# Reading GpSimd's column numbers straight from a table in memory, in a hybrid encoder block

## The chip, the cores and the metric

One core of a Trainium2 chip runs the whole kernel. The metric is the device time of one execution in microseconds; of several runs the median stands. The profile is one further execution, taken by the hardware profiler. TensorE multiplies, VectorE and ScalarE work on PSUM and SBUF, GpSimd works on SBUF, SyncE issues most transfers. Each engine has a sequencer that runs its instructions in order; register work (loads of registers, bounds checks, additions) is done by the sequencer itself.

## The reference

The kernel computes one layer of an encoder block on 512 tokens of width 2048, in float32. What matters here is its last part, a mixture of experts:

```python
h = rmsnorm(x)                                   # 512 x 2048
# top-1 of 4 groups, then top-2 of 8 experts in it: 1024 picks (token, expert, gate)
for e in range(32):                              # w_gate, w_up: 2048 x 512, w_down: 512 x 2048
    y = (silu(h[tokens_of(e)] @ w_gate[e]) * (h[tokens_of(e)] @ w_up[e])) @ w_down[e]
    x[tokens_of(e)] += gate * y
```

Before it come a combined projection, sliding-window attention, a multi-scale pool, an output projection and a cross-attention to 256 memory tokens. None of that is touched. Which tokens an expert gets is known only at run time.

## The kernel before

**Blocks.** The picks are sorted into blocks of 64 slots, block `b` for expert `b` (`SLOTS = 64`, `NE = 32`); up to 16 more blocks would take what doesn't fit, and a count `more` says how many there are. For a block, TensorE multiplies the 64 gathered columns `xsT` with gate and up (64 matmuls, `gate_up`, L2258), turns the result, and multiplies with down (32 matmuls, `down`, L2284). Two blocks make a pair; even blocks use columns 0 to 63 of `xsT` (`par` 0), odd ones 64 to 127. After a pair, a one-hot matrix spreads its results over the tokens (L2217) and VectorE adds them to the residual (L1647).

**Weights.** An expert is 6 units of 2 MB (`expert_unit`; 0 and 2 gate, 1 and 3 up, 4 and 5 down). SyncE loads each into its place in a ring as soon as TensorE has used what was there (`load_units`, L521). The fourth unit of block 0 goes, in three pieces, to buffers that only become free when the routing tables are done (`first_up`, L515, behind the semaphore `table_ready`).

**The columns.** `H` holds the normed activations, transposed: token `t` is one column of 16 values on each of 128 partitions. The gather is a copy of that column, with the token number in a register: 64 copies of 128x16 a block. For each group of 32 copies the sequencer loads 32 registers by one instruction (`TENSOR_LOAD`), then does for each register one fused operation and one bounds check (64 instructions, L695 "ISA x64" below), then issues the copies (L700, each with one more register operation). Blocks 0 and 1 are shared: ScalarE copies columns 0 to 31 (L1096), GpSimd columns 32 to 63, from `first_row`, a row of 128 token numbers that VectorE writes first (`first_ids`). From block 2 on GpSimd does all of it, alone, in a loop over pairs (L725): it fetches the pair's 128 numbers from `ids_dram`, a table in memory, to `first_row` in SBUF by a DMA (L719), waits for its landing, and does four groups of 32. Before the first copy of a block it waits until the block before the previous one has left `xsT` (`gu_copied`). TensorE's `gate_up` waits for the whole block (`block_rows`). The table itself is written once, by a DMA of GpSimd (L711), behind VectorE's `ids_ready`.

**The tables.** VectorE makes them in one sequence: the numbers of the first pair (L1597), the table `ids` (L1623), the weights of the picks (L1628), the list for blocks beyond 32 (L1631 to L1636), and copies of the gates, the last of which raises `table_ready` (L1639). TensorE fills its waits there with matmuls on constants (`keep_busy`, L1746).

Of the kernel before, what the change touches and what calls it, by code (L numbers as in the profile page):

```python
# [58 lines left out]
CUT = 3  # L59


def hybrid_block(nc, x, mem, mix_norm_g, w_in, q_norm_g, k_norm_g, sink_logits, pool_w, pool_scale,
# [5 lines left out]
    with ExitStack() as ctx:  # L68
# [104 lines left out]
        xsT = PB[:, 0:KD * P].rearrange("p (k n) -> p k n", n=P)  # L173
        first_up = [PB[:, 4096:6144], kx[:, :, :].rearrange("p h n -> p (h n)"), vx[:, :, :].rearrange("p m n -> p (m n)")]
# [3 lines left out]
        last_act_t = PB[:, 8704:8704 + KF * SLOTS]  # L178
# [45 lines left out]
        first_up_in = sem("first_up_in")  # L224
        first_used = sem("first_halves_used")
# [112 lines left out]
        pair_ids_in = sem("pair_ids_in")  # L338
# [136 lines left out]
        def _(sp):  # L475
# [34 lines left out]

            sp.wait_ge(table_ready, 1)
# [24 lines left out]
            with sp.Fori(2, NE - 2) as b:  # L536
                load_expert(b, b)
# [34 lines left out]
        def _(pool):  # L572
# [119 lines left out]
            def copy_columns(tokens, par, first, done, free=None):  # L692

                for at in range(first, SLOTS, 32):
                    _, where = nc.values_load_multi_w_load_instructions(  # L695
                        tokens[:, at:at + 32], engines=(mybir.EngineType.Pool,), min_val=0, max_val=S - 1)
                    if at == 0:
                        pool.wait_ge(gu_copied, free)
                    for j in range(32):
# [5 lines left out]
            for par in range(2):  # L705
                copy_columns(first_row[0:1, par * SLOTS:(par + 1) * SLOTS], par, 32, first_rows[par])
# [3 lines left out]
            pool.wait_ge(ids_ready, 1)  # L710
            pool.dma_start(ids_dram.rearrange("j (e s) -> (j e) s", e=2), ids[:, :]).then_inc(ids_stored, 16)  # L711
# [1028 lines left out]
        def _(pe):  # L1740
# [453 lines left out]
            def expert_landed(b, u):  # L2194
# [3 lines left out]
                else:  # L2198
# [3 lines left out]
                    if u < 2 and not (isinstance(b, int) and b < 1):  # L2202
                        loads += 1
# [220 lines left out]
```

## Time and profile before

| | us |
|---|---|
| median of 3 runs | 1741.24 (1740.82 to 1741.37) |
| the profiled execution | 1744.3 |
| its span | 1742.5 |
| mean granted TensorE clock | 0.953 |
| TensorE busy | 1530.3 (88%) |
| VectorE busy | 601.1 (34%) |
| GpSimd busy | 450.8 (26%) |
| ScalarE busy | 365.7 (21%) |

The span lies 1.8 us under the execution's own time. TensorE's busy time counts matmuls from issue to a modelled end, so 88% doesn't mean that it works at its peak. Register and DMA-issuing instructions aren't counted as busy, which matters for GpSimd: they appear as `POOLq`, its sequencer, in the chain and in the list of one line's instructions. Lines such as L695 are those of the listing above. The experts' part begins at about 686 us of the span.

### The profile page before, as it was taken

To read this page: it belongs to the slowest core of one execution; us is meant where nothing else is said; L and a number is where in the kernel's file an instruction comes from. 1 tells how busy PE (TensorE), PEld (TensorE's weight loads), DVE (VectorE), ACT (ScalarE), POOL (GpSimd) and SP (SyncE) were. 2 spreads that over 40 slices of the span, in tenths; PEclk is the share of its full clock that TensorE was granted. 3 is DMA by queue.
4 is the path that set the end of the run, shared out by engine and by line. 5 is a ranking of instruction groups with operands and counts; after the bars stand their busy time and mean duration, and the time that the engine had idled before them with its cause. 6 is when DMAs were issued, how large, how long until landed. Compare 5 with 4: busy or idle time off the path is not lost.

```text
span 1742.5 us, 25966 instructions
## 1 busy us (share of the span) xinstructions
PE 1530.3 (88%) x7008; PEld 868.5 (50%) x7008; DVE 601.1 (34%) x726; ACT 365.7 (21%) x705; POOL 450.8 (26%) x2198
## 2 busy tenths in 40 slices
PE   7999999999999998887977977977977977987977
PEld 7787777588885666232332332332332332332323
DVE  6655666632234335021221221221321231221214
ACT  6422334522222443201001001010010110010101
POOL 4560073400000000332232233233233233233230
PEclk9999999999999999998988988988999998998989
DMA  8433222542222114899999999999999998999984
GB/s 291 112 82 96 81 65 73 195 102 97 97 97 97 49 49 197 335 429 395 409 375 379 415 374 375 411 379 377 406 380 379 411 378 357 412 376 375 411 337 194
DMA packets 88922, 472.66 MB, mean 271 GB/s; under 512 B 5026, under 2 KB 43084, under 8 KB 62924
## 3 DMA queue, kind: packets, MB, share of 16 engines
q1 hardware_dynamic: 87800, 470.84, 67.8%
q0 software_dynamic: 880, 0.35, 0.4%
q14 instruction: 108, 0.88, 0.1%
q8 instruction: 34, 0.56, 0.1%
q10 hardware_dynamic: 100, 0.03, 0.0%
HBM read 466.99 MB, written 4.21 MB: 270 GB/s over the span
## 4 chain that ended last, share of the span: by engine, by line
PE 36%; POOLq 22%; issue 18%; POOL 12%; DMA 6%; DVE 4%; ACT 2%; SPq 0%; DVEq 0%; ACTq 0%
POOLq L695 20%; POOL proj_buffer L700 12%; PE ps L1965 10%; PE ps L1839 9%; DMA proj_buffer<-block_ids 4%; PE ps L2018 3%; PE ps L2258 3%; POOLq L700 1%; DMA weight_ring<-in_xkv_w_dram 1%; PE ps L1801 1%; PE ps L2348 1%; PE ps L2081 1%; ACT weight_ring L889 1%; PE ps L1894 1%; PE ps L2217 1%
## 5 line engine op out<-in xcount | busy, mean ns | idle before, releaser
L2258 PE MATMUL ps<-weight_ring,proj_buffer 128*64 128x512 f32 x2032 | 480.8, 629 | 134.6 <-POOL proj_buffer L700 134.6
L700 POOL COPY proj_buffer<-transposed_acts 128x16 f32 x1984 | 300.9, 214 | 666.1 <-issue 607.4
L2258 PEld LDWEIGHTS ps<-weight_ring,proj_buffer 128*64 128x64 f32 x2032 | 181.5, 145 | 429.0 <-issue 405.8
L1647 DVE TENSOR_TENSOR residual<-ps,residual 128x1024 f32<-128x1024 f32 x128 | 150.8, 1220 | 346.4 <-PE ps L2217 345.6
L2284 PE MATMUL ps<-weight_ring,proj_buffer 128*64 128x512 f32 x960 | 214.2, 599 | 19.5 <-DVE proj_buffer L1657 18.5
L1663 DVE SCALAR_TENSOR_TENSOR y_low<-ps,proj_buffer,y_high 64x1024 fp32r<-64x1024 f32 x60 | 77.0, 1283 | 236.7 <-ACT y_high L1082 235.7
L2284 PEld LDWEIGHTS ps<-weight_ring,proj_buffer 128*64 128x64 f32 x960 | 68.0, 138 | 148.2 <-issue 145.2
L1071 ACT ACTIVATE proj_buffer<-ps 128x512 f32<-128x512 f32 x32 | 19.1, 598 | 531.3 <-PE ps L2258 531.3
L1082 ACT ACTIVATE y_high<-ps,proj_buffer 64x1024 fp32r<-64x1024 f32 x60 | 66.5, 1109 | 289.9 <-PE ps L2284 289.2
L1839 PE MATMUL ps<-mix_high,w_in_high 128*128 128x512 f32 x288 | 117.3, 407 | 1.3 <-issue 1.3
L1839 PE MATMUL ps<-mix_high,w_in_low 128*128 128x512 f32 x288 | 112.3, 390 | 0.0
L1839 PE MATMUL ps<-normed_low,w_in_high 128*128 128x512 f32 x288 | 112.3, 390 | 0.0
L1965 PE MATMUL ps<-weight_high,mix_high 128*128 128x512 f32 x256 | 99.8, 390 | 1.0 <-issue 1.0
L1965 PE MATMUL ps<-weight_low,mix_high 128*128 128x512 f32 x256 | 99.6, 389 | 0.0
L2217 PE MATMUL ps<-y_high,spread 128*128 128x512 f32 x240 | 85.8, 439 | 9.3 <-DVE residual L1647 9.3
L1657 DVE TENSOR_TENSOR proj_buffer<-proj_buffer,ps 128x256 f32<-128x256 f32 x32 | 13.3, 416 | 197.6 <-ACT proj_buffer L1075 197.6
L2217 PE MATMUL ps<-y_low,spread 128*128 128x512 f32 x240 | 75.1, 394 | 0.0
L689 POOL MEMSET memory_values<- 128x160 f32 x1 | 0.2, 232 | 282.6 <-PE ps L2063 282.6
L1197 DVE TENSOR_TENSOR w_in_low<-weight_ring,w_in_high 128x1024 fp32r<-128x1024 f32 x36 | 48.0, 1337 | 69.7 <-ACT w_in_high L812 69.6
L2217 PEld LDWEIGHTS ps<-y_high,spread 128*128 128x128 f32 x240 | 37.0, 188 | 53.1 <-DVE residual L1647 37.1
L1360 DVE TENSOR_TENSOR weight_low<-weight_ring,weight_high 128x1024 fp32r<-128x1024 f32 x32 | 38.5, 1224 | 70.1 <-ACT weight_high L939 70.1
L1839 PEld LDWEIGHTS ps<-mix_high,w_in_high 128*128 128x128 f32 x288 | 54.1, 188 | 15.0 <-issue 3.9
(322 smaller groups left out, 1814.9 us busy)
## 6 DMA issues: line engine op xcount, KB each, us to landing
weight_ring<-in_expert_w_down_dram SPq DMA_DIRECT2D x63, 2048.0 KB, 12.1
weight_ring<-in_expert_w_gate_dram SPq DMA_DIRECT2D x62, 2048.0 KB, 10.3
weight_ring<-in_expert_w_up_dram SPq DMA_DIRECT2D x61, 2048.0 KB, 15.6
weight_ring<-in_w_in_dram SPq DMA_DIRECT2D x18, 1024.0 KB, 5.6
weight_ring<-in_w_out_dram SPq DMA_DIRECT2D x16, 1024.0 KB, 5.0
weight_ring<-in_xkv_w_dram SPq DMA_DIRECT2D x8, 1024.0 KB, 7.7
residual<-in_x_dram SPq DMA_DIRECT2D x8, 1024.0 KB, 12.9
weight_ring<-in_xq_w_dram SPq DMA_DIRECT2D x4, 1024.0 KB, 9.8
```

What stands on the lines that cost most here:

```text
L695: _, where = nc.values_load_multi_w_load_instructions(tokens[:, at:at + 32], engines=(mybir.EngineType.Pool,), min_val=0, max_val=S - 1)
L700: ins = g.tensor_copy(xsT[:, :, par * SLOTS + at + j], H[:, :, ds(where[j], 1)].rearrange("p k n -> p (k n)"))
L1082: a.activation(high[par * SLOTS:(par + 1) * SLOTS, 2 * side:2 * side + 2, :], ps[rows, 4:6, :], ACT.Copy, scale=gate[rows, ds(b, 1)]).then ...
L1197: v.tensor_tensor(in_lo[:, half], raw, in_hi[:, half].bitcast(F32), ALU.subtract).then_inc(w_lo_ready, 1)
L1647: v.tensor_tensor(part, ps[:, bank:bank + 2, :].rearrange("p b n -> p (b n)"), part, ALU.add).then_inc(signal, 1)
L1663: v.scalar_tensor_tensor(out=low[par * SLOTS:(par + 1) * SLOTS, 2 * side:2 * side + 2, :], in0=ps[rows, 4:6, :], scalar=gate[rows, ds(b, 1 ...
L1839: ins = mm(ps[:, bank, :].rearrange("p (t n) -> p t n", n=P), w_[:, half, kk, :], h_, start=(k == 0 and part == 0), stop=(k == KD - 1 and ...
L1965: ins = mm(ps[:, 4 * (n % 2) + t, :], m_, w_[:, r, kk, :], start=(u % 8 == 0 and kk == 0 and part == 0), stop=(u % 8 == 7 and kk == 1 and ...
L2018: ins = mm(ps[:, 4 + t % 2, :], H[:, k, t * P:(t + 1) * P], w[:, kk, :], start=(k == 0), stop=(k == KD - 1))
L2217: ins = mm(ps[:, bank + n, :], onehot[:, t * P:(t + 1) * P], y[:, 2 * side + n, :], start=(start and y is high), stop=(stop and y is low))
L2258: ins = mm(ps[side * SLOTS:(side + 1) * SLOTS, 0, :], xsT[:, k, par * SLOTS:(par + 1) * SLOTS], gate_up_weights(e, u, kk), start=(k == 0), ...
L2284: ins = mm(ps[half, 4 + n % 2, :], act_t[:, f * SLOTS:(f + 1) * SLOTS], w[:, n * 512:(n + 1) * 512], start=(f == 0), stop=(f == KF - 1), s ...
```

## The change

Four things change.

1. In the loop over pairs GpSimd no longer brings the numbers to SBUF. Each group of 32 loads its registers from the table in memory; the compiled program first loads the table's address, adds the offset, and loads the numbers. The semaphore `pair_ids_in` goes.
2. Columns of block 0 are shared among three engines: ScalarE 26, VectorE 12, GpSimd 26. Of block 1, ScalarE copies 28 and GpSimd 36. VectorE's 12 stand between the weights of the picks and the list for further blocks, so ahead of `table_ready`. GpSimd's store of the table moves from behind both blocks to between them.
3. Loads: the first half of block 1's first gate unit goes to a free buffer (`second_gate`) as soon as the activations are turned (`h_turned`); half of block 2's first gate unit gets a semaphore of its own, and block 2's loads are written out ahead of the loop. `last_act_t` moves to the memory of `H`.
4. `keep_busy` ahead of block 0 issues 20 matmuls on constants instead of 6.

```diff
+BY_ACT, BY_DVE = 26, 12
...
+        second_gate = PB[:, 2048:4096]
...
-        last_act_t = PB[:, 8704:8704 + KF * SLOTS]
+        last_act_t = Hf[:, 0:KF * SLOTS]
...
+            sp.wait_ge(h_turned, 56)
+            sp.dma_start(second_gate, expert_unit(1, 0)[:, 0:CHK]).then_inc(half_gate_in[0], 16)
             sp.wait_ge(table_ready, 1)
...
-            for half in range(2):
-                for u in range(2):
-                    if half == 0:
-                        sp.wait_ge(first_used, u + 1)
-                    else:
-                        sp.wait_ge(used, UE + u + 1)
-                    sp.dma_start(unit(u)[:, half * CHK:(half + 1) * CHK], expert_unit(1, u)[:, half * CHK:(half + 1) * CHK]
-                                 ).then_inc(landed[unit_slot(u)], 16)
+            sp.wait_ge(first_used, 2)
+            load_half(1, 1, 0)
+            for u in range(2):
+                sp.wait_ge(used, UE + u + 1)
+                load_half(1, u, 1)
             load_units(1, 1, (2, 4, 5))
+            sp.dma_start(unit(0)[:, 0:CHK], expert_unit(2, 0)[:, 0:CHK]).then_inc(half_gate_in[1], 16)
+            sp.wait_ge(used, 2 * 6 + (UE - 6 + 1))
+            load_half(2, 0, 1)
+            load_units(2, 2, range(1, 6))
...
             pool.wait_ge(first_ids, 1)
             pool.wait_ge(h_turned, 56)
-            for par in range(2):
-                copy_columns(first_row[0:1, par * SLOTS:(par + 1) * SLOTS], par, 32, first_rows[par])
+            copy_columns(first_row[0:1, 0:SLOTS], 0, BY_ACT + BY_DVE, first_rows[0])
+            pool.wait_ge(ids_ready, 1)
+            pool.dma_start(ids_dram.rearrange("j (e s) -> (j e) s", e=2), ids[:, :]).then_inc(ids_stored, 16)
+            copy_columns(first_row[0:1, SLOTS:2 * SLOTS], 1, 28, first_rows[1])
...
             def pair_columns(it):
-                pool.dma_start(first_row[0:1, :], ids_dram[ds(it, 1), :]).then_inc(pair_ids_in, 16)
-                landed_ids = pool.to_reg(it * 16)
-                pool.wait_ge(pair_ids_in, landed_ids)
-                block_columns(it * 2, 0)
-                block_columns(it * 2 + 1, 1)
+                for par in range(2):
+                    copy_columns(ids_dram[ds(it, 1), par * SLOTS:(par + 1) * SLOTS], par, 0, block_rows,
+                                 free=pool.to_reg(it * 2 + par - 1))
...
+            dve.wait_ge(h_turned, 56)
+            _, where = nc.values_load_multi_w_load_instructions(
+                first_row[0:1, BY_ACT:BY_ACT + BY_DVE], engines=(mybir.EngineType.DVE,), min_val=0, max_val=S - 1)
+            for j in range(BY_DVE):
+                ins = v.tensor_copy(xsT[:, :, BY_ACT + j], H[:, :, ds(where[j], 1)].rearrange("p k n -> p (k n)"))
+            ins.then_inc(first_rows[0], 1)
...
-            keep_busy(6)
+            keep_busy(20)
```

On GpSimd, at the entry of the loop over pairs, the program before reads (`gu_copied` is the wait for free columns; "ISA x64" the 64 register instructions of a group):

```order
L708 IOTA proj_buffer 128x512 [waits table_ready]
L711 DMA block_ids<-proj_buffer 48x64 [waits ids_ready]
L725 UNCONDITIONAL_BRANCH [waits ids_stored,second_block_rows]
L725 ISA
L719 DMA proj_buffer<-block_ids 1x16x8
L720 REGISTER_ALU
L716 ISA [waits pair_ids_in]
L695 TENSOR_LOAD proj_buffer
L695 ISA x64
L700 ISA [waits gu_copied]
L700 COPY proj_buffer<-transposed_acts 128x16
```

And the changed program on the same engine at the same place (its lines are numbered some ten higher, L705 for L695 and L710 for L700):

```order
L720 IOTA proj_buffer 128x512 [waits table_ready]
L730 UNCONDITIONAL_BRANCH [waits ids_stored,second_block_rows]
L730 ISA
L705 TENSOR_LOAD block_ids_ptr
L705 ISA
L705 REGISTER_ALU
L705 TENSOR_LOAD block_ids
L705 ISA x64
L710 ISA [waits gu_copied]
L710 COPY proj_buffer<-transposed_acts 128x16
```

The store L711 has left this place, and the fetch L719 with its wait is gone; the five instructions from the pointer's load to "ISA x64" stand four times in a pair's pass, where the load from SBUF and its "ISA x64" stood.

On VectorE, after the weights of the picks, the program before goes straight on to the list of further blocks:

```order
L1628 TENSOR_TENSOR proj_buffer<-proj_buffer 128x400 [waits dve_link]
L1631 TENSOR_TENSOR proj_buffer<-proj_buffer,ramp_by 128x512
L1633 TENSOR_REDUCE proj_buffer<-proj_buffer 128x16 [waits dve_link]
L1634 TENSOR_SCALAR proj_buffer<-proj_buffer 128x16 [waits dve_link]
L1635 TENSOR_SCALAR proj_buffer<-proj_buffer 128x1 [waits dve_link]
```

The changed program on VectorE, same place:

```order
L1633 TENSOR_TENSOR proj_buffer<-proj_buffer 128x400 [waits dve_link]
L1637 TENSOR_LOAD proj_buffer [waits h_turned]
L1637 ISA x24
L1640 ISA
L1640 COPY proj_buffer<-transposed_acts 128x16
```

A load of 12 registers, 24 register instructions and 12 copies have moved in ahead of the list and so ahead of `table_ready`.

## Rows read from the trace of the kernel before

**Rows 1.** The page: span, busy time (part 1), chain that ended last (part 4).

```profile
span 1742.5 us, 25966 instructions
...
PE 1530.3 (88%) x7008; PEld 868.5 (50%) x7008; DVE 601.1 (34%) x726; ACT 365.7 (21%) x705; POOL 450.8 (26%) x2198
...
PE 36%; POOLq 22%; issue 18%; POOL 12%; DMA 6%; DVE 4%; ACT 2%; SPq 0%; DVEq 0%; ACTq 0%
POOLq L695 20%; POOL proj_buffer L700 12%; PE ps L1965 10%; PE ps L1839 9%; DMA proj_buffer<-block_ids 4%; PE ps L2018 3%; PE ps L2258 3%; POOLq L700 1%; DMA weight_ring<-in_xkv_w_dram 1%; PE ps L1801 1%; PE ps L2348 1%; PE ps L2081 1%; ACT weight_ring L889 1%; PE ps L1894 1%; PE ps L2217 1%
```

**Rows 2.** Waits of the whole span: waiter, releaser; us in total, times, longest.

```profile
POOL proj_buffer L700 <- issue: 607.4, 58, 62.5
...
PE ps L2258 <- POOL proj_buffer L700: 134.6, 17, 9.8
...
POOL proj_buffer L719 <- issue: 75.2, 14, 5.7
```

**Rows 3.** Timeline of GpSimd: start, us, what; in brackets the idle time before.

```profile
720.16 0.53 POOL L719 DMA_DIRECT2D proj_buffer<-block_ids  x1 [5.16 <-DMA block_ids<-proj_buffer]
734.57 4.79 POOL L700 COPY proj_buffer<-transposed_acts 128x16 f32 x32 [13.88 <-issue]
747.79 4.79 POOL L700 COPY proj_buffer<-transposed_acts 128x16 f32 x32 [8.43 <-issue]
...
1629.62 0.48 POOL L719 DMA_DIRECT2D proj_buffer<-block_ids  x1 [5.17 <-issue]
```

**Rows 4.** The instructions of line L695: count, ns min/median/max.

```profile
L695 POOLq FUSED_REGOPS  x1984: 147/147/197, 688.5 to 1684.1; - x199
L695 POOLq SEQ_ASSERT  x1984: 18/18/32, 688.8 to 1684.3; - x199
L695 POOLq TENSOR_LOAD <-proj_buffer x62: 2021/2032/2261, 686.2 to 1675.0; - x62
```

**Rows 5.** The chain in order of time, inside two pairs: start, us, what.

```profile
728.08 0.15 POOLq L695
728.31 0.15 POOLq L695
...
783.60 0.55 issue
...
784.17 5.37 DMA proj_buffer<-block_ids
...
789.62 2.06 POOLq L695
```

**Rows 6.** The DMA view: issues of GpSimd, KB each, median us to landing.

```profile
proj_buffer<-in_router_expert_w_dram POOLq DMA_DIRECT2D x4, 64.0 KB, 6.0
proj_buffer<-block_ids POOLq DMA_DIRECT2D x15, 0.5 KB, 5.5
```

**Rows 7.** Timeline of TensorE: even and odd block of a pair, last block.

```profile
817.28 16.02 PE L2258 MATMUL ps<-weight_ring,proj_buffer 128*64 128x512 f32 x64 [8.93 <-POOL proj_buffer L700]
...
850.04 13.90 PE L2258 MATMUL ps<-weight_ring,proj_buffer 128*64 128x512 f32 x64
...
1689.30 9.99 PE L2258 MATMUL ps<-weight_ring,proj_buffer 128*64 128x512 f32 x32 [5.18 <-POOL proj_buffer L700]
```

**Rows 8.** Two stretches: length, busy us; last granted clock, DMA share, GB/s.

```profile
720.00:784.00 64.00, 59.25 (x260) 22.32 (x262) 15.61 (x15) 6.39 (x8) 19.72 (x129) 0.97 0.99 412
...
849.00:914.00 65.00, 53.59 (x234) 22.38 (x232) 15.62 (x15) 6.40 (x8) 20.10 (x130) 0.92 0.94 389
```

**Rows 9.** Instructions of lines L727 and L725: a one-register load, an addition.

```profile
L727 POOLq TENSOR_LOAD <-proj_buffer x1: 294/294/294, 1688.4 to 1688.4; - x1
...
L725 POOLq ALU_OP  x15: 43/45/49, 777.9 to 1688.2; - x15
```

**Rows 10.** Timeline: the first issue behind the finished tables.

```profile
695.53 0.33 SPq L515 DMA_DIRECT2D proj_buffer<-in_expert_w_up_dram  x1
```

**Rows 11.** The chain in order of time: the store of the table.

```profile
714.44 4.89 DMA block_ids<-proj_buffer
```

More of the change, by code:

```diff
@@ L224, in hybrid_block @@
         first_up_in = sem("first_up_in")
+        half_gate_in = [sem("second_gate_half_in"), sem("third_gate_half_in")]
         first_used = sem("first_halves_used")
@@ L524, in load_expert, with load_half @@
                 load_units(e, b, range(6))
-            for half in range(2):
-                for u in range(2):
-                    if half == 0:
-                        sp.wait_ge(first_used, u + 1)
-                    else:
-                        sp.wait_ge(used, UE + u + 1)
-                    sp.dma_start(unit(u)[:, half * CHK:(half + 1) * CHK], expert_unit(1, u)[:, half * CHK:(half + 1) * CHK]
-                                 ).then_inc(landed[unit_slot(u)], 16)
+            def load_half(e, u, half):
+                part = slice(half * CHK, (half + 1) * CHK)
+                sp.dma_start(unit(u)[:, part], expert_unit(e, u)[:, part]).then_inc(landed[unit_slot(u)], 16)
+            sp.wait_ge(first_used, 2)
[3 more added lines that the diff above has]
+                load_half(1, u, 1)
             load_units(1, 1, (2, 4, 5))
+            sp.dma_start(unit(0)[:, 0:CHK], expert_unit(2, 0)[:, 0:CHK]).then_inc(half_gate_in[1], 16)
+            sp.wait_ge(used, 2 * 6 + (UE - 6 + 1))
+            load_half(2, 0, 1)
+            load_units(2, 2, range(1, 6))
             more = sp.value_load(meta[0:1, NOVER:NOVER + 1], min_val=0, max_val=NOVER)
-            with sp.Fori(2, NE - 2) as b:
+            with sp.Fori(3, NE - 2) as b:
                 load_expert(b, b)
@@ L694, in copy_columns @@
                 for at in range(first, SLOTS, 32):
+                    n = min(32, SLOTS - at)
                     _, where = nc.values_load_multi_w_load_instructions(
-                        tokens[:, at:at + 32], engines=(mybir.EngineType.Pool,), min_val=0, max_val=S - 1)
-                    if at == 0:
+                        tokens[:, at:at + n], engines=(mybir.EngineType.Pool,), min_val=0, max_val=S - 1)
+                    if at == 0 and free is not None:
                         pool.wait_ge(gu_copied, free)
-                    for j in range(32):
+                    for j in range(n):
                         ins = g.tensor_copy(xsT[:, :, par * SLOTS + at + j], H[:, :, ds(where[j], 1)].rearrange("p k n -> p (k n)"))
@@ L1091, in _ @@
             act.wait_ge(hT_ready, 56)
-            for par in range(2):
+            for par, n in enumerate((BY_ACT, 28)):
                 _, where = nc.values_load_multi_w_load_instructions(
-                    first_row[0:1, par * SLOTS:par * SLOTS + 32], engines=(mybir.EngineType.Activation,), min_val=0, max_val=S - 1)
-                for j in range(32):
+                    first_row[0:1, par * SLOTS:par * SLOTS + n], engines=(mybir.EngineType.Activation,), min_val=0, max_val=S - 1)
+                for j in range(n):
                     ins = a.activation(xsT[:, :, par * SLOTS + j], H[:, :, ds(where[j], 1)].rearrange("p k n -> p (k n)"), ACT.Copy)
@@ L2195, in expert_landed @@
                 s = unit_slot(u)
+                if isinstance(b, int) and b in (1, 2) and u == 0:
+                    pe.wait_ge(half_gate_in[b - 1], 16)
                 if isinstance(b, int) and b == 0 and u == 3:
@@ L2201, in expert_landed @@
                         loads -= 1
-                    if u < 2 and not (isinstance(b, int) and b < 1):
+                    if u == 1 and not (isinstance(b, int) and b < 1):
                         loads += 1
@@ L2206, in gate_up_weights @@
             def gate_up_weights(b, u, kk):
+                if isinstance(b, int) and b == 1 and u == 0 and kk < 4:
+                    return second_gate.rearrange("p (k n) -> p k n", n=FF)[:, kk, :]
                 if isinstance(b, int) and b == 0 and u == 3:
```

7 lines of the change are left out of this document (1 added, 6 removed).

## The prediction

> **What bounds the kernel now.** I read the page's chain first: half of what ended last (22% POOLq, 12% POOL, 18% issue) runs over GpSimd's register work and its 16-element copies (L695, L700) [rows 1]. The waits agree: before its copies GpSimd was idle 607.4 us for "issue", so its own sequencer held it and nobody else, and TensorE waited 134.6 us for those copies, in 17 waits [rows 2]. That is a bound by one in-order instruction stream, though the engine is busy only 26% of the span. Its rhythm is in the timeline: the loop over pairs of blocks issues its fetch of token numbers at 720.16 and the fifteenth time at 1629.62, so a pair takes (1629.62 - 720.16) / 14 = 64.96 us, and four groups of 32 copies stand in it, 13.2 us apart (the first two of the 60 are shown) [rows 3].
>
> What fills 13.2 us: one load of 32 registers, 2.03 us (the median of 62); then for each register a fused operation and a bounds check, and such couples start 0.227 us apart, 7.26 us for 32; then the issue of 32 copies, the remaining 3.9 us [rows 4, 5]. What is left of a pair, 64.96 - 52.8 = 12.2 us, is about 6.1 us for the fetch (783.60 to 789.62 in the chain, issue and landing together) and 5 to 6 us at the jump back, the "issue" wait before L719 (75.2 us in 14) [rows 2, 5].
>
> Who stands behind it: TensorE idles 8.93 us before the even block of a pair, until the last copy [rows 7]; its own pair is thus 64.96 - 8.9 = 56 us. The weights of a pair are 12 units of 2.097 MB, 25.17 MB; where the DMA share was 0.99 they came at 412 GB/s, so they need 61.1 us [rows 8]. So GpSimd has only 4 us of lead over the DMA: that is all a faster GpSimd can win for a pair, while every microsecond by which it gets slower is paid in full, 15 times. From its last copy (1689.2) to the end of the span are 53.3 us, with TensorE starting at that copy [rows 1, 7].
>
> **The change, part by part.** The pair loop comes first. Removed: the fetch, 6.1 us, and four loads from SBUF, 4 x 2.03 = 8.1 us; 64.96 - 14.2 = 50.8 us stay (checks, copies, jump back). Added four times, once for each group of 32: a load of the pointer to the table, one register operation and one addition (0.147 + 0.045 = 0.2 us by the like of them [rows 4, 9]) and a load of 32 registers out of memory. So the pair becomes 50.8 + 4 x (P + 0.2 + L), with P for the pointer (two registers, I take it) and L for the 32.
>
> The trace shows no register load from memory, so L is bounded. Low: memory answers like SBUF, L = 2.03. High: each register costs a whole load of one register, 0.294 us [rows 9], L = 32 x 0.294 = 9.4. Between them, what does one register add? From SBUF (2.03 - 0.294) / 31 = 0.056 us, and the load grows with the number, so it isn't one burst; from memory each step has further to go. Midway between 0.056 and 0.294 is 0.175, L = 0.294 + 31 x 0.175 = 5.7. The nearest row for the trip itself is the fetch of the same 512 bytes of the same table by DMA: 5.5 us to landing [rows 6]. The two lie together, and I take L = 5.6 and P = 0.294 + 0.175 = 0.47 (0.35 to 0.59). Each group then adds 6.27, a pair takes 50.8 + 25.1 = 75.9 us, 10.9 more than now, and 15 pairs 164 us more. Does memory get slower under the weights' traffic? A GpSimd DMA took 6.0 us to land in the quiet stretch (router weights) and 5.5 in the busy one [rows 6], so I add nothing.
>
> The Trainium skill, "Runtime: NRT & Kernel Launch", section "Instruction fetch mechanics", speaks against the change: it puts a register load at about 200 ns for each register even in bulk, because each is an uncached round trip. By that page as an estimate L would be 6.4 and P 0.4, the pair 78.8 us and the kernel some 1943 us. The load from SBUF, 56 ns for each further register, is far cheaper than that, so the rule can only hold for memory; no run here shows it yet.
>
> The start. In the first pair GpSimd loads 26 registers instead of 32, checks and copies 26: six fewer at 0.056 + 0.227 + 0.15 is 2.6 us. For the second block it copies 36 in two loads instead of 32 in one: 4 more, some 2 us. The store of the table is issued between the two, some 15 us before it is needed, in place of after both, where the loop waited 4.89 us for its landing [rows 11]. GpSimd's loop can then begin at about 714 in place of 719.5: 5.5 us gained. That holds if the first entry to the loop costs nothing new; a jump back costs 5 to 6 us, now hidden at the entry behind the store's landing, so the gain may be 0.
>
> VectorE now loads 12 registers, checks them and copies 12 columns before it goes on to `table_ready`: 0.9 + 2.7 + 12 x 0.2 = 6 us by GpSimd's rows, so `table_ready` comes at about 701 instead of 695.5, and with it the last 2 MB of block 0, issued at 695.53 [rows 10]. TensorE starts block 0 some 3 us sooner and may wait for that unit in its middle. I cost all of this at nothing: block 0 and block 1 end long before block 2's columns are there (752.6 now, the end of the second group [rows 3]), so TensorE reaches the same wait for GpSimd. Nor does the iota behind `table_ready` move, GpSimd gets there at 713. The early megabyte of block 1, the split loads of blocks 1 and 2 and the longer warm-up of TensorE fall under the same cover. If GpSimd were fast, each could be worth or cost up to some 5 us.
>
> The tail is unchanged: TensorE already waits 5.18 us for the very last columns [rows 7].
>
> **Sum.** 15 x 10.9 - 5.5 = +158 us. The profiled execution took 1744.3 (span 1742.5 and 1.8 around it), the median of the runs is 1741.24; the difference goes on the median: 1900 us.
>
> **Rivals.** *A: memory is nearly as near as SBUF.* L = 2.03, P = 0.35: a pair of GpSimd is 50.8 + 10.3 = 61.1 us, level with the weights' 61.1; 15 x 3.9 + 5.5 = 63 us less, 1678 us. It decides where a group costs under (65.3 - 50.8) / 4 = 3.6 us, that is L under 3.0 (87 ns for a register). For it: the fetch and the wait for it are gone, and one load in one instruction may stream. Against: the load is dear per register even from SBUF, and half of the fetch's price must be met four times over. Chance 0.17, and 0.02 more for L so close to 3.0 that nothing is seen.
>
> *B: each register is a full load of its own.* L = 9.4, P = 0.59: the pair is 50.8 + 40.8 = 91.6 us, 26.6 more; 1741 + 400 - 5.5 = 2135 us, or above. For it: the checks and loads of the sequencer show no overlap anywhere. Against: from SBUF the 32 cost a fifth of that. Chance 0.16, of which 0.05 lies above 2150.
>
> *C: my forecast*, L from 3.3 to 8, a pair of 67 to 86 us: 0.65. It is the likeliest.
>
> **Numbers.** About 0.2% is what a measurement of this kernel can tell from no change. Faster 0.17, same 0.02, slower 0.81. The range leaves out A and the top of B: from 1760 (L = 3.3) to 2150 (B with its bound).
>
> **What would show it.** The groups of 32 copies, now 13.2 us apart, should stand at about 17.4 us (11.2 + 6.3); at 13.7 A is right, at 21 B. The load from the table should read near 5.6 us and the pointer's load near 0.5. The loop should start near 714; at 719 its entry costs a fetch of instructions. TensorE's wait before an even block should grow from 8.9 to some 15 to 20 us with a new one before the odd block, since its columns come 35 us after the even ones and TensorE is through the even block in 33 (817.28 to 850.04) [rows 7]; the DMA share should fall from 0.94 [rows 8] to about 0.8. I am wrong if the load takes under 3 us, or if the four groups are not in line behind each other because the sequencer loads ahead while the engine copies: the copies' 3.9 us of issue are all such a lead could hide.

## The result and the profile after

The changed kernel takes 2206.26 us (median of 4 runs, 2203.64 to 2209.91) against 1741.3 us; the ratio is 1.267, with a 95% interval of 1.265 to 1.269. It is slower, as forecast, but by 465 us where 158 were forecast, and outside the range.

The page of the kernel after, its span, busy time and chain, answers to [rows 1]:

```profile
span 2202.4 us, 26116 instructions
...
PE 1563.2 (71%) x7036; PEld 902.8 (41%) x7036; DVE 604.5 (27%) x738; ACT 364.7 (17%) x695; POOL 444.8 (20%) x2181
...
POOLq 42%; PE 27%; issue 15%; POOL 10%; DVE 3%; ACT 1%; DMA 1%; SPq 0%; DVEq 0%; ACTq 0%
```

No engine's busy time has moved by more than 35 us. GpSimd's sequencer (`POOLq`) has grown from 22% of the chain to 42%, some 540 us more, and transfers have shrunk from 6% to 1%, some 80 us less (estimates from whole per cents): together that is the loss. The waits of the kernel after (waiter, releaser, us in total, times, longest), which answer to [rows 2]:

```profile
POOL proj_buffer L710 <- issue: 1214.0, 63, 63.3
...
PE ps L2274 <- POOL proj_buffer L710: 562.9, 31, 26.6
```

TensorE now waits before nearly every block, 31 times, where it waited 17 times before. GpSimd's timeline over one pair after, and the first group of the next, in place of [rows 3]:

```profile
826.64 5.04 POOL L710 COPY proj_buffer<-transposed_acts 128x16 f32 x32 [14.02 <-issue]
856.74 4.81 POOL L710 COPY proj_buffer<-transposed_acts 128x16 f32 x32 [25.06 <-issue]
873.02 4.82 POOL L710 COPY proj_buffer<-transposed_acts 128x16 f32 x32 [11.47 <-issue]
900.51 4.81 POOL L710 COPY proj_buffer<-transposed_acts 128x16 f32 x32 [22.66 <-issue]
919.28 5.04 POOL L710 COPY proj_buffer<-transposed_acts 128x16 f32 x32 [13.96 <-issue]
```

That is the surprise: the groups don't stand evenly. Two of the four intervals are long (30.1 and 27.5 us) and two short (16.3 and 18.8). In each of the fifteen passes the second and fourth load from the table are long, and from the second pass on the first and third are short; from 826.64 to 1686.86 nine pairs take 95.6 us each. The load instructions of L705 (ns min/median/max), which answer to [rows 4] and [rows 9]:

```profile
L705 POOLq TENSOR_LOAD <-block_ids_ptr x60: 1050/2841/5024, 715.9 to 2122.0; - x60
...
L705 POOLq TENSOR_LOAD <-block_ids x60: 3663/9236/17642, 717.8 to 2126.4; - x60
```

The same instruction with the same 32 registers takes 3.7 us or 17.6. Two of them in the chain of the kernel after, in order of time (start, us):

```profile
741.54 14.63 POOLq L705
...
768.56 4.01 POOLq L705
```

And the stretches in which they lie, with a third around the load of 14.75 us that began at 834.55 (the last three numbers are granted clock, DMA share and GB/s), beside [rows 8]:

```profile
741.00:756.00 15.00, 10.33 (x50) 3.19 (x44) 2.61 (x4) 3.20 (x4) 0.00 (x0) 0.97 1.01 429
768.50:772.60 4.10, 4.10 (x12) 1.34 (x14) 0.00 (x0) 0.00 (x0) 0.00 (x0) 0.56 0.03 8
837.00:849.50 12.50, 0.96 (x6) 0.07 (x2) 2.57 (x2) 2.22 (x2) 0.00 (x0) 0.64 0.98 421
```

The long loads lie where the weights come in at 420 GB/s, the short ones where the DMA engines stand still. This holds for all 60 loads from the table: the 29 with a DMA share under 0.2 during the load took 3.66 to 4.02 us, the 30 with one over 0.9 took 10.8 to 17.6 us, and the one between them 7.7. The engines stand still because the ring is full: at 768.5 TensorE, which had waited 15.5 us for GpSimd's columns, has only just begun its block, and SyncE issues the next unit at 777.5. Over a longer stretch the DMA share has fallen from the 0.94 of [rows 8] to 0.65 (720 to 1600 us).

### The profile page after: what moved, and what is told of

It is laid out like the page before. It is cut to its first block, busy times and chain, and to the rows that moved or that the text cites. A ratio compares the mean times of both kernels' runs of the same rounds, so it can differ in the third digit from the quotient of the medians.

```text
span 2202.4 us, 26116 instructions
## 1 busy us (share of the span) xinstructions
PE 1563.2 (71%) x7036; PEld 902.8 (41%) x7036; DVE 604.5 (27%) x738; ACT 364.7 (17%) x695; POOL 444.8 (20%) x2181
## 4 chain that ended last, share of the span: by engine, by line
POOLq 42%; PE 27%; issue 15%; POOL 10%; DVE 3%; ACT 1%; DMA 1%; SPq 0%; DVEq 0%; ACTq 0%
POOLq L705 41%; POOL proj_buffer L710 10%; PE ps L1977 8%; PE ps L1851 7%; PE ps L2030 2%; POOLq L710 1%; PE ps L1813 1%; DMA weight_ring<-in_xkv_w_dram 1%; PE ps L2274 1%; PE ps L2364 1%; PE ps L2093 1%; ACT weight_ring L894 1%; PE ps L1906 1%; PE ps L2090 1%; PE ps L2091 1%
## 5 line engine op out<-in xcount | busy, mean ns | idle before, releaser
L2274 PE MATMUL ps<-weight_ring,proj_buffer 128*64 128x512 f32 x2024 | 509.4, 659 | 562.9 <-POOL proj_buffer L710 562.9
L2274 PEld LDWEIGHTS ps<-weight_ring,proj_buffer 128*64 128x64 f32 x2024 | 208.1, 152 | 859.4 <-issue 775.7
L710 POOL COPY proj_buffer<-transposed_acts 128x16 f32 x1982 | 301.9, 215 | 1214.0 <-issue 1214.0
L2300 PE MATMUL ps<-weight_ring,proj_buffer 128*64 128x512 f32 x960 | 214.1, 598 | 19.5 <-DVE proj_buffer L1669 18.5
L2300 PEld LDWEIGHTS ps<-weight_ring,proj_buffer 128*64 128x64 f32 x960 | 72.7, 138 | 143.3 <-issue 140.4
L1202 DVE TENSOR_TENSOR w_in_low<-weight_ring,w_in_high 128x1024 fp32r<-128x1024 f32 x36 | 48.1, 1337 | 69.5 <-ACT w_in_high L817 69.5
L1851 PEld LDWEIGHTS ps<-normed_low,w_in_high 128*128 128x128 f32 x288 | 54.1, 188 | 12.6 <-issue 2.2
L1851 PEld LDWEIGHTS ps<-mix_high,w_in_low 128*128 128x128 f32 x288 | 54.1, 188 | 11.4
```

The source lines that it names most:

```text
L710: ins = g.tensor_copy(xsT[:, :, par * SLOTS + at + j], H[:, :, ds(where[j], 1)].rearrange("p k n -> p (k n)"))
L1202: v.tensor_tensor(in_lo[:, half], raw, in_hi[:, half].bitcast(F32), ALU.subtract).then_inc(w_lo_ready, 1)
L1851: ins = mm(ps[:, bank, :].rearrange("p (t n) -> p t n", n=P), w_[:, half, kk, :], h_, start=(k == 0 and part == 0), stop=(k == KD - 1 and ...
L2274: ins = mm(ps[side * SLOTS:(side + 1) * SLOTS, 0, :], xsT[:, k, par * SLOTS:(par + 1) * SLOTS], gate_up_weights(e, u, kk), start=(k == 0), ...
L2300: ins = mm(ps[half, 4 + n % 2, :], act_t[:, f * SLOTS:(f + 1) * SLOTS], w[:, n * 512:(n + 1) * 512], start=(f == 0), stop=(f == KF - 1), s ...
```

## The experiments

Theory T is: the loss is the register loads from memory, and the weights' reading stretches them. It was set against rivals one by one. All times of runs are medians, or the time of a single run where no interval stands beside them; the ratios are to the kernel before on the same chip.

**Which part of the change costs.** The first kernel puts the loop over pairs back, with numbers in SBUF, and keeps the rest of the change:

```diff
             def pair_columns(it):
-                for par in range(2):
-                    copy_columns(ids_dram[ds(it, 1), par * SLOTS:(par + 1) * SLOTS], par, 0, block_rows,
+                pool.dma_start(first_row[0:1, :], ids_dram[ds(it, 1), :]).then_inc(pair_ids_in, 16)
+                landed_ids = pool.to_reg(it * 16)
+                pool.wait_ge(pair_ids_in, landed_ids)
+                for par in range(2):
+                    copy_columns(first_row[0:1, par * SLOTS:(par + 1) * SLOTS], par, 0, block_rows,
```

> The changed kernel with its loop over pairs put back as before: one DMA of 128 numbers to SBUF a pair and four loads of 32 registers from SBUF. What is left of the change is the sharing of the first blocks, the early megabyte, the split loads and the longer warm-up. Theory T (the register loads from memory, stretched by the weights' traffic, are the whole loss): about 1736 us, the 5.5 us of the earlier loop start gained, at worst 1741; loads of 2.03 us in the loop. Rival R1 (the first blocks or the new loads of weights also cost something): over 1750 us.

Measured: 1739.66 us, ratio 0.998 (0.997 to 0.9996). The second makes the opposite cut, only the loop of the change in the kernel before:

> The kernel before with only its loop over pairs changed, so that the registers are loaded from the table in memory; the first blocks stay as they were. Theory T: all of the loss is here, 2206 + 5 = about 2210 us, within 15; a pair of 95 to 96 us. Rival R1 (a part of the loss comes from the first blocks or the new loads): under 2190 us.

Measured: 2202.86 us, ratio 1.266 (1.261 to 1.270). So the loss is in the loop, all of it, and the other three parts of the change are worth some 2.5 us of gain. R1 falls.

**Is it the traffic?** The changed kernel, its units of weights cut to a sixteenth from block 3 to block 29 (the products of these blocks are wrong by that, the token numbers are made before and stay):

```diff
             with sp.Fori(3, NE - 2) as b:
-                load_expert(b, b)
+                for u in range(6):
+                    sp.wait_ge(used, b * 6 + (UE - 6 + u + 1))
+                    sp.dma_start(unit(u)[:, 0:256], expert_unit(b, u)[:, 0:256]).then_inc(landed[unit_slot(u)], 16)
```

> The changed kernel, in whose loop each 2 MB unit of weights of blocks 3 to 29 is cut to its first 256 columns, a sixteenth of the bytes; the rest of the weights is left out. Theory T (each register is a trip to memory, and the weights' traffic stretches it): all loads from the table fall to the 3.7 us, and the pointer's to the 1.06 us, that they took where the DMA engines happened to be idle; a pair is then 50.8 + 4 x (1.06 + 0.2 + 3.7) = 70.6 us and the kernel about 2206 - 14 x 25 = 1855 us. Rival R2 (the loads are slow for another reason, such as the place in the loop or GpSimd's own instruction fetch): loads of 12 to 17 us stay in groups 2 and 4 of a pair, and the time stays over 2100 us.

Measured: 1836.36 us. Its load instructions from 850 to 1600 us, where the DMA share was 0.08:

```profile
L707 POOLq TENSOR_LOAD <-block_ids_ptr x44: 1063/1075/1317, 854.2 to 1585.3; - x44
...
L707 POOLq TENSOR_LOAD <-block_ids x44: 3691/3828/4126, 855.5 to 1586.6; - x44
```

All 44 take 3.7 to 4.1 us, none is long, with the same instructions in the same places of the loop. In the first and the last pair, where whole units are still loaded, the same kernel has loads of 17.6, 15.7 and 13.3 us. R2 falls. The kernel that fills the weights' places from SBUF has full DMA engines, but reads no memory with them:

```diff
             with sp.Fori(3, NE - 2) as b:
-                load_expert(b, b)
+                for u in range(6):
+                    sp.wait_ge(used, b * 6 + (UE - 6 + u + 1))
+                    sp.dma_start(unit(u), Hf[:, 0:2 * CHK]).then_inc(landed[unit_slot(u)], 16)
```

> The changed kernel, in whose loop every unit of weights of blocks 3 to 29 is filled with 2 MB from the transposed activations in SBUF instead of from memory: the same number of DMAs and bytes on the same DMA engines, but no reading of memory; the products of these blocks are left wrong by it. If it is the reading of memory that stretches the register loads (theory T in its narrow form): loads near 3.7 us throughout, as with little traffic. Rival R3 (it is the DMA engines' traffic on the way to and from SBUF that they share, wherever it comes from): loads of 10 us and more remain while the DMA engines are busy, 3.7 where they are idle.

Measured: 1966.7 us, now bound by those transfers (28.6 us from issue to landing for 2 MB). Its DMA share and its table loads, 850 to 1600 us:

```profile
850.00:1600.00 750.00, 579.61 (x2151) 213.29 (x2147) 144.29 (x139) 58.18 (x73) 187.80 (x1244) 0.87 0.99 313
...
L707 POOLq TENSOR_LOAD <-block_ids x38: 3690/3795/3997, 859.7 to 1580.7; - x38
```

At a DMA share of 0.99 no load is over 4.0 us. R3 falls as well: what a register load shares with the weights is the reading of memory, not the DMA engines and not the way into SBUF, as far as 313 GB/s can show it (the weights come at 420). Whether it is the memory itself or the path out of it, these two runs don't tell.

**What is the unit of a load?** The groups were cut (`step=8`, later 12 and 6, in place of 32 in the loop):

```diff
-            def copy_columns(tokens, par, first, done, free=None):
+            def copy_columns(tokens, par, first, done, free=None, step=32):
...
-                                 free=pool.to_reg(it * 2 + par - 1))
+                                 free=pool.to_reg(it * 2 + par - 1), step=8)
```

> The changed kernel with the groups of its loop over pairs cut from 32 registers to 8: 16 pointer loads and 16 table loads a pair in place of 4 and 4, the same 128 registers. Theory T, trip by trip (a load costs a start and then a share for each register): where the DMA engines are idle a table load of 8 takes about 1.06 + 6 x 0.087 = 1.6 us, a quarter of 3.7 plus the start; under the weights' reading about 4.5 to 6 us, and the kernel gets slower, over 2300 us, since 12 more pointer loads of 1 to 5 us stand in each pair. Rival R4 (a load pays one long trip, whatever the number of registers): a load of 8 takes as long as one of 32, 3.7 and 12 to 17 us, and the kernel is over 3000 us.

Measured: 2557.97 us. A table load of 8 takes 1.13 us in the median, that is at rest, and 4.1 to 5.2 under traffic: R4 is out, but so is the expected 1.6 us, and the pointer with its two registers takes nearly as long as eight registers. Of the guess that memory is read by eights, the next run asked:

> The changed kernel with groups of 12 registers in the loop (5 of 12 and one of 4 for a block). The groups of 8 gave 1.12 us at rest where the pointer's 2 registers took 1.06, and 32 took 3.7 to 3.8: so a register isn't a trip of its own. Theory T2 (a load reads memory in portions of 8 registers, each one trip of about 0.9 to 1.1 us at rest and 3 to 4.6 us under the weights' reading, one after another): loads of 12 take two trips, 1.9 to 2.1 us at rest and 6 to 9 us under traffic; those of 4 take 1.1. Rival R7 (a start of 1.0 us and then a share that grows evenly beyond 8 registers, 0.11 us each): 1.55 us at rest.

Measured: 2417.65 us. Three table loads of its chain, of 4 and of 12 registers at rest, and of 12 under traffic (start, us):

```profile
1000.40 0.69 POOLq L705
...
1003.75 1.55 POOLq L705
...
1021.09 5.46 POOLq L705
```

1.55 us is R7's number, and T2's portions of eight are refuted; but R7's start of 1.0 us isn't right either, since four registers take 0.69. 4, 8, 12 and 32 registers lie on one line, 0.25 + 0.109 us for each, which still leaves two readings:

> The changed kernel with groups of 6 registers in the loop (10 of 6 and one of 4 for a block). At rest loads of 4, 8, 12 and 32 registers took 0.68, 1.12, 1.56 and 3.7 to 3.8 us: 0.24 + 0.109 for each register. Theory S (each register is a trip of its own): 6 registers take 0.24 + 0.65 = 0.90 us at rest. Rival R10 (memory is read in portions of 4 registers, 0.44 us each): 6 registers take two portions, 1.12 us.

Measured: 3125.03 us; no time had been forecast. Four loads of six registers in a row, in its chain, at rest:

```profile
1002.96 1.51 POOLq L705
...
1007.78 2.74 POOLq L705
...
1013.89 1.52 POOLq L705
...
1019.00 2.81 POOLq L705
```

Neither 0.90 nor 1.12. But the alternation has a key: groups of six start at bytes 0, 24, 48, 72 of the row, so by turns on a multiple of 16 bytes and off it. Let a load start with 0.25 us and take its registers in fours, counted from its own first one; let a four that begins on a multiple of 16 bytes come in one trip to memory, about 0.43 us at rest, and every other register in a trip of its own. Then 32 aligned registers are 8 trips, 0.25 + 8 x 0.435 = 3.7 (measured 3.7); 12 are 3 trips, 1.55 (1.55); six from an aligned start are one trip of four and two of one, 1.5 (1.51); six from a start 8 bytes off are six trips, 2.8 (2.74); the pointer's two registers are two trips, 1.1 (1.06). All five fit these two numbers. (That the fours are counted from the load's own start is part of the fit: in the six from 8 bytes off, the last four registers do fill an aligned 16 bytes, and still it takes six trips.) The cost of 3125 us fits in kind, with more trips and 22 pointers a pair; it wasn't worked out.

The rule was formed behind these runs, and no run was made to test it. But the changed kernel holds a test that nobody looked for. At its first pair three engines load registers from `first_row` in SBUF: ScalarE 26 and 28, from bytes 0 and 256; VectorE 12, from byte 104, which is 8 off a multiple of 16; GpSimd 26, from byte 152, also 8 off, and then 32 and 4, from bytes 368 and 496 (count, ns min/median/max):

```profile
L705 POOLq TENSOR_LOAD <-proj_buffer x3: 331/2057/6004, 684.7 to 713.4; - x3
...
L1098 ACTq TENSOR_LOAD <-proj_buffer x2: 1739/1938/2137, 684.7 to 695.6; - x2
...
L1637 DVEq TENSOR_LOAD <-proj_buffer x1: 2981/2981/2981, 691.0 to 691.0; - x1
```

GpSimd's 4 and 32 aligned registers took 0.33 and 2.06 us, so a trip to SBUF is (2.06 - 0.33) / 7 = 0.25 us and the start 0.08. By the rule the 26 off the mark are 26 trips, 6.5 us (6.00), VectorE's 12 are 12 trips, 3.0 us (2.98), and ScalarE's aligned 26 and 28 are 8 and 7 trips, 2.1 and 1.8 us (2.14, 1.74). ScalarE's 26 were loaded at the same moment as GpSimd's 26 and took a third as long, so it isn't the company of other engines. The part of the rule that reads alignment holds for SBUF as well, on sizes on which it wasn't formed.

Under the weights' reading 32 registers took 10.8 to 17.6 us; a load of 14.6 is (14.6 - 0.25) / 8 = 1.8 us a trip, the range 1.3 to 2.2, three to five times the trip at rest.

**Does it hang on where the table lies?** The table was stored a second time, some 33 MB further on, for the odd blocks:

```diff
+    far_ids = nc.dram_tensor("far_ids", (65536, 2 * SLOTS), I32, kind="Internal").ap()[65536 - NBLK // 2:65536, :]
...
-                    copy_columns(ids_dram[ds(it, 1), par * SLOTS:(par + 1) * SLOTS], par, 0, block_rows,
+                    copy_columns((ids_dram, far_ids)[par][ds(it, 1), par * SLOTS:(par + 1) * SLOTS], par, 0, block_rows,
```

> The changed kernel with the table stored twice, the second time over 33 MB further on in memory; groups 1 and 2 of a pair (even block) load from the first, groups 3 and 4 (odd block) from the second. In one of four runs the change without checks was as fast as if its loads weren't stretched at all. Rival R11 (it hangs on where the table lies in memory against the weights): loads of one table stay near 3.7 us also where the DMA engines are busy, the other's don't, or the runs fall apart into two times over 3% from each other. Otherwise (traffic alone): groups 2 and 4 both read 10 to 17 us where the DMA engines are busy, 2206 us within 20.

Measured: 2209.73 us (2205.29 to 2214.51), ratio 1.269. In its chain, a load from the near table (932.47) and one from the far table (980.38), both with the DMA engines busy:

```profile
932.47 15.63 POOLq L706
...
980.38 14.11 POOLq L706
```

Both are long, and the runs lie together. The fourth load of a pair, from the far table, took 10.9 to 14.3 us over the fifteen passes, where in the changed kernel, from the near table, it took 10.8 to 15.0. At these two places the position makes no difference.

**A shorter pair, more contention.** The change with GpSimd's fused operations and bounds checks left out:

```diff
-                        tokens[:, at:at + n], engines=(mybir.EngineType.Pool,), min_val=0, max_val=S - 1)
+                        tokens[:, at:at + n], engines=(mybir.EngineType.Pool,), min_val=0, max_val=S - 1,
+                        skip_runtime_bounds_check_because="the table is clamped to S - 1 where it is written")
```

> The whole change, its registers loaded from memory, with GpSimd's couples of fused operation and bounds check left out. If the loads kept the durations that they have in the changed kernel, a pair would take 95.6 - 29 = 67 us, 1775 us in all. Theory T (each trip is stretched by the weights' reading): the shorter pair leaves the DMA engines less idle, so more of the four loads fall into busy stretches and get from 3.7 to 12 us and more; a pair of 70 to 85 us, 1820 to 2000 us, and hardly any load at 3.7. Rival R9 (the duration hangs on the load's place in the pair, not on the traffic): 1775 us, groups 1 and 3 still at 3.7.

Measured: 1841.45, 1841.95 and 1844.99 us, and once 1644.89. In the trace of the run of 1844.99 us the table loads have a median of 12.6 us, up from 9.2, and the longest takes 23.9:

```profile
L705 POOLq TENSOR_LOAD <-block_ids x60: 3707/12550/23923, 711.1 to 1772.8; - x60
```

From 720 to 1600 us the DMA share was 0.86, up from 0.65. So T holds against R9: 29 us of sequencer work fell away from a pair, but the time fell by only 364 us of the 435 that 15 pairs would give, since the loads met more traffic and got longer: those of a pair, pointers included, took 56.5 us on average, up from 47.6. That hardly any would stay at 3.7 us didn't come true: the third of a pair still took under 4 us in eleven of the fifteen passes. The single run of 1645 us fits none of this; the same kernel once more:

> The kernel of the twelfth run once more, unchanged, in more rounds: registers from memory and no checks, of which three runs took 1841 to 1845 us and one 1645. It tells how often the fast one comes. If traffic alone stretched the loads, GpSimd's pair could not be under the weights' 58.8 us while the DMA engines are always busy: 4 x (3 + 0.05 + 12) + 22 = 82 us; so the run of 1645 us must have had loads under 9 us on average in full traffic, and something besides the traffic has a say. Expected if that depends on the execution: again some runs near 1645; if it was a single accident: all of 1841 to 1845.

Measured: 1838.62 to 1851.0 us, median 1847.86, ratio 1.060 (1.058 to 1.063), none near 1645. Its trace repeats the other one, at a DMA share of 0.85:

```profile
L705 POOLq TENSOR_LOAD <-block_ids x60: 3664/12099/23382, 715.4 to 1776.7; - x60
```

One execution in eight took 1645 us. It wasn't a profiled one, and what was different in it stays open. It limits T: 1645 us is the time of the kernels below that the weights bind, with DMA engines that never rest. A pair without its loads is some 16 us (72.3 - 56.5), so to stay under the weights' 58.9 a pointer and its load would have to take under 11 us together in full traffic (an estimate), where they averaged 14.1 in the trace, quiet stretches included. So traffic stretches the loads in every trace on record, but it isn't the only thing that sets by how much.

**What the kernel could do instead.** First the fetch of the numbers by DMA, but a pair ahead, when the last 32 are in registers:

```diff
+            def fetch_ids(it):
+                pool.dma_start(first_row[0:1, :], ids_dram[ds(it, 1), :]).then_inc(pair_ids_in, 16)
...
                     if at == 0 and free is not None:
                         pool.wait_ge(gu_copied, free)
+                    if at + n == SLOTS and ahead is not None:
+                        ahead()
```

> The changed kernel without loads from memory in the loop: the pair's 128 numbers come to SBUF by one DMA as before, but it is issued for the next pair when the last 32 numbers of this one are in registers, so that the trip lies beside the copies and the jump back. GpSimd's pair is then 64.96 - 6.1 + 0.5 = 59.4 us, the weights' 61.1 us take over as the bound: about 1739.7 - 15 x 3.9 = 1681 us. Rival R5 (what GpSimd gains is taken back elsewhere, for instance because the trip isn't hidden): over 1725 us, pairs of 64 us.

Measured: 1701.53 us, ratio 0.976 (0.974 to 0.978), between the theory's 1681 and R5. The fetches stand 59.6 us apart at 828.92 and 888.47, which is GpSimd's pair as worked out, but over all fourteen intervals from 769.22 on they stand 59.1 to 64.7 apart, 61.6 on average. In the chain GpSimd is all but gone:

```profile
PE 62%; DMA 26%; DVE 6%; ACT 2%; issue 2%; POOL 1%; POOLq 1%; SPq 0%; DVEq 0%; ACTq 0%
```

The weights could come in 58.9 us a pair (below) and GpSimd could do it in 59.6. That the pair is longer than either, since with two bounds so close now one and now the other waits, is likely and not shown. Over 880 us the DMA share is 0.97 at 403 GB/s. The same in the kernel before:

> The kernel before with the fetch issued a pair ahead and nothing else of the change (the last block's activations move to the buffer that the change gives them). About 1742 - 58 = 1684 us if the weights' reading binds from then on. Against the kernel with the first part too it tells what the first part is worth once GpSimd no longer binds: nothing if both read 1681 to 1684, up to 5 us either way if the first blocks' loads decide.

Measured: 1700.05 us, ratio 0.975 (0.973 to 0.977), the same: the first part of the change adds nothing to it. And with the 32 couples of register instructions a group left out:

> As the kernel that fetches a pair ahead, and GpSimd's 32 couples of fused operation and bounds check a group are left out (the table holds only values up to 511): 7.26 us less for each of four groups, GpSimd's pair some 30 us. If the weights' reading binds already (61.1 us a pair), the time stays that of the kernel with checks, 1681 us, within 0.3%. Rival R6 (GpSimd still binds after the fetch ahead): another 15 to 60 us faster.

Measured: 1644.06 us, ratio 0.944 (0.941 to 0.946), faster than the theory (1681), as R6 said. The windows of both, 720 to 1600 us, first with and then without the checks:

```profile
720.00:1600.00 880.00, 777.81 (x3272) 303.38 (x3274) 219.17 (x211) 90.53 (x114) 282.43 (x1838) 0.96 0.97 403
```

```profile
720.00:1600.00 880.00, 809.59 (x3502) 323.86 (x3503) 230.98 (x224) 97.00 (x122) 300.00 (x1932) 0.98 1.00 427
```

Without the checks the DMA engines never rest and bring 427 GB/s: 25.17 MB in 58.9 us. The 61.1 us of the prediction came from a stretch at 412 GB/s and a share of 0.99 and was no limit. Then the checks alone, in the kernel before and with the first part of the change:

> The kernel before, in which only GpSimd's couples of fused operation and bounds check are left out, 32 a group. GpSimd's pair is then about 64.96 - 29 = 36 us, well under the weights' 58.8 us (25.17 MB at the 428 GB/s seen where GpSimd no longer binds). So the weights bind: 1644 us plus whatever the first part of the change is worth. Theory W (weights bind, the fetch ahead is needless without checks): 1644 to 1652 us. Rival R8 (the fetch of the numbers still shows): over 1660 us.

> The first part of the change (shared first blocks, early megabyte, split loads, warm-up), the loop over pairs as before with registers from SBUF, and GpSimd's couples of fused operation and bounds check left out. Theory W: 1644 us, the time of the kernel that also fetched ahead. The difference to the kernel before without checks is what the first part is worth once the weights bind: by the earlier start of the weights' loads (one megabyte is 2.4 us at 428 GB/s) 2 to 5 us faster; rival: nothing.

Measured: 1642.32 us (ratio 0.942, 0.941 to 0.943) and 1643.44 us (0.943, 0.941 to 0.944). The window of the first of them:

```profile
720.00:1600.00 880.00, 809.78 (x3500) 315.09 (x3498) 230.52 (x223) 97.46 (x122) 298.57 (x1934) 0.98 1.00 426
```

W holds: with the checks gone the weights bind in all three, the fetch ahead is needless, and the first part of the change is worth nothing; the 2 to 5 us expected for it weren't there. The kernel before with one argument changed is as fast as any, 101 us faster than it was. The checks guard against a wrong number; VectorE already clamps the numbers to the last token where it writes them (`ALU.min` in L1597 and L1623), and the kernel without the checks relies on that.

## Why the prediction was wrong

- **What bounds the kernel** was right: the chain, the 64.96 us of a pair, the four equal groups, the 53 us behind the last copy (52.0 after). The direction followed from it, and the two cut kernels confirm that nothing outside the loop weighs. The loads do stand in line with the copies and nothing hides them.
- **The bound behind GpSimd** was put at 61.1 us a pair; it is 58.9. That didn't touch the forecast, nor rival A, whose own GpSimd pair was 61.1 as well; it put the expectation for the kernel without checks, 1681 us, some 37 us too high. A stretch with a share of 0.99 isn't a stretch at the limit when GpSimd also binds in it.
- **L at rest** was put at 5.6 us, from 0.175 us a register. It is 3.7: four aligned registers come in one trip of 0.43 us. The midpoint between two rows was a guess, and too high; by luck it took some of the error below back.
- **P** was put at 0.47 us. It is 1.06 at rest and 4.0 and 4.1 in the two busy groups of the pair at 814 us: two registers that aren't an aligned four are two whole trips.
- **The step that failed** is "Does memory get slower under the weights' traffic? ... so I add nothing". With the weights' reading nearly gone the loads took 3.7 to 4.1 us and the kernel 1836 us, inside the range; in the changed kernel, under that reading, they took 10.8 to 17.6. In the pair from 814.28 to 906.89 the loads of the table took 3.67, 14.75, 3.86 and 12.00 us and those of the pointer 1.06, 3.98, 1.07 and 4.15: 44.5 us, against 4 x (0.47 + 5.6) = 24.3 in the sum. Over all fifteen pairs the average is 47.6 us; at the prices at rest it would be 4 x (3.7 + 1.06) = 19.0. So traffic added 28.6 us a pair, which the sum had at nothing, L and P took 5.3 too many, and what stays of a pair 3.5 too many (below): a pair came to 95.8 us instead of 75.9, and 15 x 19.9 = 298 of the 307 us that were missing.
- **The row it rested on**, 5.5 us for a DMA in traffic against 6.0 in quiet [rows 6], was the wrong row. The two don't compare, 0.5 KB against 64 KB. And a landing holds one wait for memory, or a few side by side, beside much else, while a load of 32 makes eight one behind the other; that is an argument, no run measured the same DMA with and without traffic.
- **What stays of a pair** was put at 50.8 us. With the pointer's 0.8 us of register work it came to 92.6 - 44.5 = 48.1 instead of 51.6. In the chain the "issue" before the next pair is 1.5 us after, where it was 4.48 before: the jump back is shorter where the DMA engines are idle. With the weights' places filled from SBUF, at a DMA share of 0.99, it is 3.3 to 5.9 us again. Without the checks a pass of the loop has 275 instructions of GpSimd instead of 531, and the last copy and the next pair's first load stand under 0.05 us apart, in traffic too. The Trainium skill, "Runtime: NRT & Kernel Launch", section "Instruction fetch mechanics", says that a branch to a page that isn't held waits for a DMA that fetches it. The traces agree that the gap depends on traffic and on the length of the loop; they don't show the fetch itself.
- **The start**: GpSimd's iota ended at 716.2 and the first pointer load began at 715.9, where 714 was forecast. The entry cost no fetch. GpSimd's 26 registers, put at less than 2.03 us, took 6.00, and VectorE's 12, put at 0.9, took 2.98: both loads begin 8 bytes off a multiple of 16. VectorE's part was worked out as 6 us and took from 691.0 to 699.3; SyncE issued the last unit of block 0 at 701.87 instead of 695.53. All of it lay under GpSimd's loop, as said: 2.5 us of gain in the run with the loop put back, not 5.5.
- **The range** ended at 2150 because rival B took a one-register load from SBUF, 0.294 us, as the dearest thing a register could cost. A bound for memory can't come from a row of SBUF: 14.75 us for 32 registers is 0.46 each.
- **The page's figure.** The Trainium skill's 200 ns a register ("Runtime: NRT & Kernel Launch", section "Instruction fetch mechanics") came nearer than my sum, with 1943 us, and is right neither at rest nor in traffic: 0.109 us at rest where four come together, 0.41 for a single one, 0.45 under traffic even for aligned fours. The Trainium skill, "Advanced Engine Details and Errata", section "Network/Comms", gives memory latency as 0.2 us on average and 2 us or more at high load. The longer trips under traffic, 1.8 to 2.2 us, agree with its second number; at rest the trip reads 0.43.

## What to carry to other kernels

Where a sequencer's work is the bound, count its register instructions first: here 64 of them for each group of 32 copies were 29 of 65 us, and leaving them out gave 101 us, where fetching the numbers a pair ahead gave 41. Keep token numbers in SBUF and load registers there, from starts on 16 bytes; a load from memory is a chain of round trips, each of which pays for whatever else reads memory, so price it in traffic and not at rest. A trip's price under load can't be read from a DMA's landing, and a bound for an operation that isn't in the trace needs a row of the same path, or has to be left wide open.

## What wasn't expected of the hardware

- A register load from memory takes 3.7 us for 32 registers at rest and 10.8 to 17.6 us while DMAs read 420 GB/s from memory; up to 23.4 us in the kernel without checks, at a DMA share of 0.85. DMAs from SBUF at a share of 0.99 and 313 GB/s leave it at 3.8.
- Alignment decides its price: six registers took 1.51 us from a start on 16 bytes, 2.74 us from a start 8 bytes off.
- So it does in SBUF: GpSimd took 2.06 us for 32 registers from a start on 16 bytes and 6.00 us for 26 from a start 8 bytes off. The change's split of 26, 12 and 26 columns put two of its three loads on such starts.
- One execution in eight of the kernel with loads from memory and no checks took 1645 us in place of 1839 to 1851.
